# Block transposes on VectorE for one of the two forms of a triangular inverse, in place of matmuls

## The chip, the cores and the metric

The kernel runs on one core of one Trainium2 chip. The metric is the device time of one execution, in microseconds; 2361.78 us is the median of three runs of the kernel before. Most executions agree within 0.3%.

## What is computed

One inference step of a two-layer backbone. Each layer has a token mixer of three branches and a gated ConvFFN, over 128 context tokens and 256 latent tokens, 1024 channels wide, all in fp32. The change lies in the first branch, RWKV-7 time mixing, whose recurrence per head and direction is:

```
def step(S, inp):
    r_t, w_t, k_t, v_t, a_t, b_t = inp
    sa = jnp.einsum('bhvk,bhk->bhv', S, a_t)
    S = S * w_t[:, :, None, :] + sa[..., None] * b_t[:, :, None, :] + v_t[..., None] * k_t[:, :, None, :]
    return S, jnp.einsum('bhvk,bhk->bhv', S, r_t)
```

The kernel computes it in chunks of 64 tokens. Within a chunk the terms `sa` depend on each other through a strictly triangular 64x64 matrix L (products of `a_t` with earlier `b_s`, decayed), and what is needed is the inverse X = (I - L)^-1 for every chunk, head and direction. For the backward direction the triangle is the other one.

## The kernel before

**Stages.** The layer loop runs twice. In it, four head pairs `p` are worked through one after the other (the pair stage, about 137 us each), then come the merge, the output projection and the FFN as dense matmuls with split operands. Each engine has its own program, written in the order in which it runs; semaphores named in `PER` join them (`at_of(name, p, i)` is the i-th signal of that name in pair p). Nothing is reordered by a scheduler.

**Layout of the inverse.** A pair holds 2 heads (`hb`) x 6 combinations of direction and token tile (`x`) x 2 chunks (`c`), so 24 matrices of 64x64. The two chunks stand on the two halves of the 128 partitions. `xv` is X, `tvv` is its transpose, both `[128, hb, x, 64]` in SBUF, one `hb` being 128x384. `au[..., 0, 0:CH]` holds the transposed L after masking. `gg` is a scratch tile.

**The inverse by levels.** X starts as the identity. Level 0 writes the neighbours of the diagonal, and level `lv` (1 to 5, `LEVELS` = 6) joins diagonal blocks of size 2^lv into blocks of twice the size. For each level PE makes G = L X (`gl`, 24 matmuls, into PSUM), ACT copies it to `gg`, PE makes X G (side 0, `xt`) and its transpose G^T X^T (side 1), 24 matmuls each, and VectorE writes the new off-diagonal blocks into `xv` and `tvv` by a predicated copy (`pred`, L1210), one for each side and `hb`. Level 5 makes only side 1, since only `tvv` is read afterwards. For level 0 PE makes the not transposed L by 24 more matmuls (`l_done`), and GpSimd fills both `xv` and `tvv` with identities (L1553, L1554).

**What stands around it on each engine.** PE's order in a pair is: the products `am` (48 matmuls, masked by VectorE into `au`), the 24 for L, `attend(4)` of the attention branch, 24 for `g0`, then for each level: `gl`; other work (`attend`, transposes, and in levels 4 and 5 `retain` and `ada_steps`); then `xt`. So in time an `xt` group stands directly before the `gl` of the next level, which needs its result. VectorE runs `attend(4 + lv)` (or `retain(lv - 4)`) and then the four predicated copies of a level. ACT copies `gl` results, then its part of `attend`.

PE waits ahead of `gl` of level `lv`, for each `hb`, on the predicated copy of side 1 of the level before: index `4 * (lv - 1) + 2 * hb + 1` of `x_ready`.

**How the trace counts.** An fp32 matmul stands in the trace as two MATMUL records, so that the 24 + 24 + 24 matmuls of `xt` and the next `gl` are "x144". `settle()` makes an engine wait for its own previous instruction.

Of the kernel before, what the change touches and what calls it, by code (L numbers as in the profile page):

```python
# [27 lines left out]
P = 128  # L28
# [8 lines left out]
CH = 64  # L37
# [4 lines left out]
LEVELS = 6  # L42
# [33 lines left out]
for _name, _n in (("ident", 128), ("ones", 128), ("blk", 128), ("perm", 128), ("cos", 256), ("sin", 256),  # L76
# [6 lines left out]
PER = {  # L83
    "kk_rk": 1, "kk_sq": 1, "kkn_done": 1, "bon_done": 1, "bon_used": 1, "kkn_root": 1, "kk_ready": 1,
    "lw_done": 2, "la_done": 2, "sig_ready": 4, "scan_ready": 2, "lx_ready": 2, "exp_ready": 6, "kd_ready": 2,
    "til_ready": 2, "rr_ready": 2, "pend_ready": 2, "bkp_ready": 2, "dg_ready": 1, "x_init": 2, "bias_ready": 1,
    "vt_done": 1, "vt_ready": 1,
    "am_done": 6, "au_ready": 6, "l_done": 2, "x_ready": 22, "g0_done": 2, "g0_ready": 2,
    "gl_done": 10, "gl_ready": 10, "xt_done": 18, "wm_done": 2, "wm_ready": 2, "u_done": 2, "u_ready": 2,
    "mi_done": 2, "mi_ready": 2, "nn_done": 2, "nn_ready": 4, "qh_done": 2, "qh_ready": 4,  # L90
    "ch_done": 3, "ch_ready": 3, "yv_done": 2, "y_done": 2, "y_copied": 4, "yc_ready": 1, "ysq_ready": 1, "gn_done": 2,
    "yroot_ready": 1, "o_ready": 1,
# [41 lines left out]
def trunk(nc, xin, wstream, prm_d, pk_d, cc_d, const_d, x_out, nak, nav, srw, srt):  # L134
    ctx = ExitStack()
    with ctx:
# [151 lines left out]
        def sem(name):  # L288
# [9 lines left out]
            bias_ready bkp_ready bon_done bon_used c_ready ch_done ch_ready  # L298
            de_ready dg_ready dt_ready exp_ready g0_done g0_ready g_hi g_lo gelu_ready
            gl_done gl_ready gn_done h_hi h_lo h_ready half_used hnorm kd_ready kk_ready  # L300
            kk_rk kk_sq kkn_done kkn_root kt_done kt_ready l_done la_done lora_in lp_exp
            lw_done lx_ready m_hi m_lo mi_done mi_ready mod_ready mrg_ready mx_ready nn_done
            nn_ready no_done no_ready o_ready out_k out_st p_ready p_step pend_ready pk_in
            pn_ready prm_in pt_done pt_ready qh_done qh_ready qx_ready rgn_done ro_ready
            rope_done rope_ready row_done row_ready rows_clear rr_ready rroot_ready rsq_ready
            rst_done rst_ready rt_root ry_done ry_ready ryc_ready s_ready sc_done scan_ready
            sctx_ready sd_ready sig_ready silu_c sq_ready sq_used ss_done st0_ready st_done
            til_ready u_done u_ready v_step vt_done vt_ready w_hi w_lo w_used wm_done wm_ready
# [22 lines left out]
        with nc.Fori(0, DEPTH) as layer:  # L331
            with nc.Block() as block:
# [25 lines left out]
                def at_of(name, p, i):  # L358

                    return S[name].h, PER[name] * p + i + 1  # L360
# [4 lines left out]
                def hc(c):  # L365
                    return slice(CH * c, CH * c + CH)
# [44 lines left out]
                def _(pe):  # L411
                    used = [0]

                    def mm(out, a, b, start=True, stop=True, sig=None):
                        ins = nc.tensor.matmul(out, a, b, start=start, stop=stop, skip_group_check=True)  # L415
                        if sig:
                            S[sig].by(ins)
                        elif used[0]:
                            S["w_used"].by(ins, used[0])
                            used[0] = 0  # L420
# [79 lines left out]
                    for p in range(PAIRS):  # L500
# [125 lines left out]
                        for q in range(3):  # L626
# [5 lines left out]
                            for x in (2 * q, 2 * q + 1):  # L632
                                d, t = x // 3, x % 3
                                for k in range(2):
                                    for c in range(2):
                                        for hb in range(2):
# [1 line left out]
                                            mm(psw[hc(c), b, a:a + 128].rearrange("p (e i) -> p e i", e=2),  # L638
                                               bk[rows(hb), d, k, tok(t, c)], ar[rows(hb), d, :, tok(t, c)],
                                               sig="am_done" if (x % 2, k, c) == (1, 1, 1) else None)  # L640
                        pe.wait_ge(*at_of("au_ready", p, 3))
                        for x in range(6):
                            d, t = x // 3, x % 3
                            for c in range(2):
                                for hb in range(2):
                                    mm(psw[hc(c), 2 + hb, CH * x:CH * x + CH], ar[rows(hb), d, 0, tok(t, c)],
                                       bk[rows(hb), d, 0, tok(t, c)], sig="l_done" if (x, c) == (5, 1) else None)
                        attend(4)
                        for hb in range(2):
                            pe.wait_ge(*at_of("au_ready", p, 4 + hb))  # L650
# [4 lines left out]

                        for lv in range(1, LEVELS):
                            for hb in range(2):
                                pe.wait_ge(*at_of("x_ready", p, 4 * (lv - 1) + 2 * hb + 1))
                                for x in range(6):
                                    for c in range(2):  # L660
                                        mm(psw[hc(c), g_bank(lv, hb), CH * x:CH * x + CH], au[hc(c), hb, x, 0, 0:CH],
                                           xv[hc(c), hb, x, :], sig="gl_done" if (x, c) == (5, 1) else None)
                            if lv == 1:
                                attend(5)
                                for d in range(2):
                                    flipped(zb + 13 + d, [ar[:, d, 0, TT[t]:TT[t] + P] for t in range(3)])
                                pe.wait_ge(*at_of("g0_ready", p, 1))
                            elif lv in (2, 3):
                                d = lv - 2
                                attend(lv + 4)  # L670
                                pe.wait_ge(*at_of("bkp_ready", p, d))
                                for k in range(2):
                                    flipped(zb + 15 + 2 * d + k, [bkp[:, d, k, t * P:t * P + P] for t in range(3)])
                            else:
                                retain(lv - 4)
                                ada_steps(2)
                            for hb in range(2):
                                pe.wait_ge(*at_of("gl_ready", p, 2 * (lv - 1) + hb))
                                for side in range(1 if lv == LEVELS - 1 else 0, 2):
                                    b = g_bank(lv, hb) if side else x_bank(lv, hb)  # L680
                                    a_, b_ = (gg, tvv) if side else (tvv, gg)
                                    for x in range(6):
                                        for c in range(2):
                                            mm(psw[hc(c), b, CH * x:CH * x + CH], a_[hc(c), hb, x, :],
                                               b_[hc(c), hb, x, :], sig="xt_done" if (x, c) == (5, 1) else None)

                        freed(zb + 13)
                        freed(zb + 14)
                        for hb in range(2):
                            pe.wait_ge(*at_of("x_ready", p, 20 + hb))  # L690
# [499 lines left out]
                def _(dve):  # L1190
# [18 lines left out]
                    def pred(out, mask, data, sig):  # L1209
                        L.do(V.copy_predicated(out, mask, data), S[sig])  # L1210

                    def normed(j):

# [84 lines left out]
                    for p in range(PAIRS):  # L1298
# [91 lines left out]
                        for q in range(3):  # L1390
                            for hb in range(2):
# [7 lines left out]
                        dve.wait_ge(*at_of("x_init", p, 1))  # L1399
                        L.settle()  # L1400
                        for hb in range(2):
                            dve.wait_ge(*at_of("l_done", p, hb))
                            pred(by_dir(xv[:, hb]), level_mask(0, 0), by_dir_of(2 + hb), "x_ready")
                            pred(by_dir(tvv[:, hb]), level_mask(0, 1), by_dir(au[:, hb, :, 0, 0:CH]), "x_ready")
                        attend(4)
                        for lv in range(1, LEVELS):
                            if lv < 4:
                                attend(4 + lv)
                            else:
                                retain(lv - 4)  # L1410
                            for hb in range(2):
                                for side in range(1 if lv == LEVELS - 1 else 0, 2):
                                    i = 16 + hb if lv == LEVELS - 1 else 4 * (lv - 1) + 2 * hb + side
                                    dve.wait_ge(*at_of("xt_done", p, i))
                                    pred(by_dir((tvv if side else xv)[:, hb]), level_mask(lv, side),
                                         by_dir_of(g_bank(lv, hb) if side else x_bank(lv, hb)), "x_ready")
                            if lv == 2:
                                for hb in range(2):
                                    i = 8 + 2 * p + hb
                                    ts(dtab[:, hb, :], cv("posd", 384), lg[:, i:i + 1])  # L1420
                                    L.settle()
                                    stt(dtab[:, hb, :], cv("negd", 384), lg[:, i + 8:i + 9], dtab[:, hb, :], op1=ALU.add,
                                        sig="dt_ready")
# [96 lines left out]
                def _(pool):  # L1520
# [11 lines left out]
                    for p in range(PAIRS):  # L1532
# [17 lines left out]
                        pool.wait_ge(*at_of("til_ready", p, 1))  # L1550
                        eye = cv("eye", CH)
                        L.settle()
                        L.do(G.tensor_copy(xv.rearrange("p h x c -> p (h x) c"), eye.unsqueeze(1).to_broadcast([P, 12, CH])), S["x_init"])  # L1553
                        L.do(G.tensor_copy(tvv.rearrange("p h x c -> p (h x) c"), eye.unsqueeze(1).to_broadcast([P, 12, CH])), S["x_init"])  # L1554
                        pool.wait_ge(*at_of("pend_ready", p, 1))
                        for d in range(2):
# [172 lines left out]
```

## Time and profile before

| | us |
|---|---|
| median of 3 runs | 2361.78 (2360.79 to 2362.64) |
| the profiled execution | 2359.16 |
| its span, first to last instruction | 2357.4 |
| PE busy in the span | 2103.2 (89%) |
| VectorE busy | 968.0 (41%) |
| ACT busy | 855.0 (36%) |
| GpSimd busy | 661.6 (28%) |
| mean granted TensorE clock | 0.959 |

PE is the busiest engine by far, and its gaps are short. The share alone doesn't tell what one stage is limited by: the pair stage alternates between dense matmuls and chains of small steps in which PE, ACT and VectorE hand results on. Such chains are read in the timelines of the engines side by side. "Idle before" in a timeline row names the engine whose work ended that gap.

### The profile page before, as it was taken

The numbers are of one execution on the slowest core, as the hardware profiler recorded it, in microseconds if no ns is written. First come the engines' busy times: TensorE is split into PE (matmuls) and PEld (weight loads), VectorE is DVE, ScalarE is ACT, GpSimd is POOL, SyncE is SP. The second block draws the span as 40 slices with busy tenths as digits, with TensorE's granted clock in tenths as the row PEclk, the third lists the DMA queues.
The fourth block names the chain that finished last, engine by engine and source line by source line (L and its number), as shares of the span: only waits on it lengthen the run. The fifth ranks groups of instructions, "written<-read, shape, count | busy, mean of one in ns | idle before, by whom it ended". The sixth has DMA issues, their size and how long they took to land. (4 is left out here: it accounts for less than half of the span.)

```text
span 2357.4 us, 44798 instructions
## 1 busy us (share of the span) xinstructions
PE 2103.2 (89%) x18904; PEld 1696.5 (72%) x18904; DVE 968.0 (41%) x1589; ACT 855.0 (36%) x1668; POOL 661.6 (28%) x390
## 2 busy tenths in 40 slices
PE   4889999998799979999649899999987999799994
PEld 0566575756599959999615766757575999599994
DVE  2344435444443245650214444445545322455502
ACT  2342433334333344443133423333343333544431
POOL 0110202011155525555202002020201555255551
PEclk9999999999899979999879999999998999899997
DMA  6313222131233313333043131221312333133330
GB/s 239 105 38 116 66 77 97 39 116 38 88 121 122 120 54 118 125 124 125 18 174 117 36 112 61 92 91 56 100 38 93 117 125 120 59 120 124 123 125 27
DMA packets 64421, 227.37 MB, mean 96 GB/s; under 512 B 7264, under 2 KB 11616, under 8 KB 63840
## 3 DMA queue, kind: packets, MB, share of 16 engines
q1 hardware_dynamic: 58464, 215.60, 27.8%
q10 hardware_dynamic: 5760, 8.92, 1.2%
q8 instruction: 152, 2.49, 0.4%
q14 instruction: 45, 0.37, 0.1%
HBM read 220.81 MB, written 3.68 MB: 95 GB/s over the span
## 5 line engine op out<-in xcount | busy, mean ns | idle before, releaser
L415 PE MATMUL psz<-part 128*128 128x386 f32 x5280 | 959.3, 343 | 53.0 <-DVE part L1198 51.0
L415 PEld LDWEIGHTS psz<-part 128*128 128x128 f32 x5280 | 942.9, 191 | 66.0 <-issue 46.1
L1525 POOL TENSOR_TENSOR part<-ring,part 128x1024 fp32r<-128x1024 f32 x220 | 528.7, 2404 | 574.0 <-ACT part L856 574.0
L415 PE MATMUL psz<-hbuf,ring 128*128 128x386 f32 x1344 | 451.7, 493 | 31.7 <-issue 29.3
L415 PE MATMUL psw<-work 64*64 64x64 f32 (+5 forms) x10944 | 434.5, 234 | 31.2 <-issue 16.9
L415 PEld LDWEIGHTS psw<-work 64*64 64x64 f32 (+3 forms) x10944 | 381.0, 139 | 108.6 <-issue 80.7
L415 PEld LDWEIGHTS psz<-hbuf,ring 128*128 128x128 f32 x1344 | 254.2, 191 | 217.8 <-issue 39.5
L856 ACT ACTIVATE part<-ring 128x1024 fp32r<-128x1024 f32 x220 | 231.5, 1053 | 172.2 <-PE psz L415 155.8
L856 ACT ACTIVATE work<-psw 128x384 f32<-128x384 f32 (+6 forms) x360 | 129.6, 388 | 294.1 <-PE psw L415 248.6
L1525 POOL TENSOR_TENSOR work<-work 128x386 f32<-128x386 f32 (+1 forms) x48 | 42.6, 895 | 448.9 <-DVE work L1198 437.7
L1204 DVE SCALAR_TENSOR_TENSOR mix<-psz,prm,mix 128x385 f32<-128x385 f32 x176 | 109.0, 619 | 138.2 <-ACT mix L856 135.1
L1198 DVE TENSOR_TENSOR part<-mix,part 128x386 fp32r<-128x386 f32 x84 | 128.9, 1555 | 67.5 <-ACT part L856 67.5
L856 ACT ACTIVATE mix<-psz 128x386 f32<-128x386 f32 x96 | 47.3, 493 | 258.0 <-PE psz L415 252.8
L1207 DVE RECIPROCAL rstd<-rstd 128x386 f32<-128x386 f32 x8 | 20.5, 2564 | 265.0 <-ACT rstd L856 265.0
L1210 DVE COPY_PREDICATED work<-const,psw 128x384 f32<-128x384 uint32 x160 | 94.3, 591 | 76.6 <-PE psw L415 65.6
L856 ACT ACTIVATE mix<-psz,prm 128x386 f32<-128x386 f32 x88 | 51.4, 585 | 201.7 <-DVE mix L1198 104.5
L856 ACT ACTIVATE work<-psz 128x386 f32<-128x386 f32 (+2 forms) x160 | 75.7, 499 | 130.9 <-PE psz L415 127.5
L1198 DVE TENSOR_TENSOR work<-psw,work 128x256 f32<-128x256 f32 (+3 forms) x128 | 45.9, 395 | 152.8 <-PE psw L415 152.8
L1525 POOL TENSOR_TENSOR pk<-pk,const 128x768 f32<-128x768 f32 x8 | 14.6, 1826 | 290.2 <-DMA pk<-in_pk 290.2
L856 ACT ACT_TABLE_LOAD x58 | 74.4, 1283 | 49.6 <-issue 27.0
L415 PE MATMUL psw<-ring,small 128*2 128x512 f32 x128 | 35.1, 654 | 59.7 <-DMA ring<-in_w 59.2
L1198 DVE TENSOR_TENSOR mix<-psz,mix 128x386 f32<-128x386 f32 x48 | 26.7, 559 | 145.6 <-PE psz L415 145.5
(89 smaller groups left out, 1341.1 us busy)
## 6 DMA issues: line engine op xcount, KB each, us to landing
ring<-in_w SPq DMA_DIRECT2D x400, 512.0 KB, 3.5
pk<-in_pk ACTq DMA_DIRECT2D x8, 832.0 KB, 4.5
const<-in_const SPq DMA_DIRECT2D x1, 2307.0 KB, 8.2
xres<-in_x SPq DMA_DIRECT2D x1, 1544.0 KB, 11.2
out_x<-xres SPq DMA_DIRECT2D x1, 1544.0 KB, 5.1
out_nak<-work ACTq DMA_DIRECT2D x8, 64.0 KB, 1.5
out_nav<-work ACTq DMA_DIRECT2D x8, 64.0 KB, 1.5
out_srt<-work ACTq DMA_DIRECT2D x8, 64.0 KB, 1.5
```

Source lines behind the costliest of these rows:

```text
L415: ins = nc.tensor.matmul(out, a, b, start=start, stop=stop, skip_group_check=True)
L856: L.do(nc.scalar.activation(out, src, f, **kw), S[sig] if sig else None, free)
L1198: L.do(V.tensor_tensor(out, a, b, op), *sig_of(sig, free))
L1204: L.do(V.scalar_tensor_tensor(out, a, s_, b, op0, op1), *sig_of(sig, free))
L1207: L.do(V.reciprocal(out, a), *sig_of(sig, None))
L1210: L.do(V.copy_predicated(out, mask, data), S[sig])
L1525: L.do(G.tensor_tensor(out, a, b, op), S[sig] if sig else None)
```

## The change

The matrices L in not transposed form and the transposed products of levels 1 to 4 are no longer made by PE. In levels 0 to 4 the two forms are block diagonal with blocks of at most 32x32, and VectorE's transpose instruction turns every 32x32 block of a 128x384 tile in place of its block position. `flip` is that instruction. Level 0 now writes `tvv` by a predicated copy from `au` and makes `xv` by a flip; levels 1 to 4 write `xv` by a predicated copy and make `tvv` by a flip. Each flip waits for the copy ahead of it (`L.settle()`). Level 5 is as before but for its PSUM bank. A new semaphore `tv_ready` says that `tvv` is written, and `x_ready` that `xv` is; PE waits for `x_ready` ahead of `gl` and for `tv_ready` ahead of `xt`. GpSimd fills one tile with identities instead of two.

```diff
@@ PE
-                        pe.wait_ge(*at_of("au_ready", p, 3))
-                        for x in range(6):
-                            d, t = x // 3, x % 3
-                            for c in range(2):
-                                for hb in range(2):
-                                    mm(psw[hc(c), 2 + hb, CH * x:CH * x + CH], ar[rows(hb), d, 0, tok(t, c)],
-                                       bk[rows(hb), d, 0, tok(t, c)], sig="l_done" if (x, c) == (5, 1) else None)
...
-                                pe.wait_ge(*at_of("x_ready", p, 4 * (lv - 1) + 2 * hb + 1))
+                                pe.wait_ge(*at_of("x_ready", p, 2 * (lv - 1) + hb))
...
-                                for side in range(1 if lv == LEVELS - 1 else 0, 2):
-                                    b = g_bank(lv, hb) if side else x_bank(lv, hb)
-                                    a_, b_ = (gg, tvv) if side else (tvv, gg)
-                                    for x in range(6):
-                                        for c in range(2):
-                                            mm(psw[hc(c), b, CH * x:CH * x + CH], a_[hc(c), hb, x, :],
-                                               b_[hc(c), hb, x, :], sig="xt_done" if (x, c) == (5, 1) else None)
+                                if lv > 1:
+                                    pe.wait_ge(*at_of("tv_ready", p, 2 * (lv - 2) + hb))
+                                a_, b_ = (gg, tvv) if lv == LEVELS - 1 else (tvv, gg)
+                                for x in range(6):
+                                    for c in range(2):
+                                        mm(psw[hc(c), x_bank(lv, hb), CH * x:CH * x + CH], a_[hc(c), hb, x, :],
+                                           b_[hc(c), hb, x, :], sig="xt_done" if (x, c) == (5, 1) else None)
@@ VectorE
+                    def flip(out, a, sig):
+
+                        L.do(V.transpose(out.rearrange("p x c -> p (x c)"), a.rearrange("p x c -> p (x c)")), S[sig])
...
-                            dve.wait_ge(*at_of("l_done", p, hb))
-                            pred(by_dir(xv[:, hb]), level_mask(0, 0), by_dir_of(2 + hb), "x_ready")
-                            pred(by_dir(tvv[:, hb]), level_mask(0, 1), by_dir(au[:, hb, :, 0, 0:CH]), "x_ready")
+                            pred(by_dir(tvv[:, hb]), level_mask(0, 1), by_dir(au[:, hb, :, 0, 0:CH]))
+                            L.settle()
+                            flip(xv[:, hb], tvv[:, hb], "x_ready")
...
-                                for side in range(1 if lv == LEVELS - 1 else 0, 2):
-                                    i = 16 + hb if lv == LEVELS - 1 else 4 * (lv - 1) + 2 * hb + side
-                                    dve.wait_ge(*at_of("xt_done", p, i))
-                                    pred(by_dir((tvv if side else xv)[:, hb]), level_mask(lv, side),
-                                         by_dir_of(g_bank(lv, hb) if side else x_bank(lv, hb)), "x_ready")
+                                dve.wait_ge(*at_of("xt_done", p, 2 * (lv - 1) + hb))
+                                if lv == LEVELS - 1:
+                                    pred(by_dir(tvv[:, hb]), level_mask(lv, 1), by_dir_of(x_bank(lv, hb)), "tv_ready")
+                                    continue
+                                pred(by_dir(xv[:, hb]), level_mask(lv, 0), by_dir_of(x_bank(lv, hb)), "x_ready")
+                                L.settle()
+                                flip(tvv[:, hb], xv[:, hb], "tv_ready")
@@ GpSimd
-                        L.do(G.tensor_copy(xv.rearrange("p h x c -> p (h x) c"), eye.unsqueeze(1).to_broadcast([P, 12, CH])), S["x_init"])
```

VectorE from the `am` masks of a pair to `attend(4)`, before. COPY_PREDICATED is `pred`, TENSOR_TENSOR 128x512 the masking into `au`, RECIPROCAL the start of `attend(4)`:

```order
L1198 TENSOR_TENSOR work<-psw,const 128x512 x6
L1210 COPY_PREDICATED work<-const,psw 128x384
L1210 COPY_PREDICATED work<-const,work 128x384
L1210 COPY_PREDICATED work<-const,psw 128x384
L1210 COPY_PREDICATED work<-const,work 128x384
L1207 RECIPROCAL small<-small 128x1
```

The same place now; STREAM_TRANSPOSE is `flip`:

```order
L1191 TENSOR_TENSOR work<-psw,const 128x512 x6
L1203 COPY_PREDICATED work<-const,work 128x384
L1207 STREAM_TRANSPOSE work<-work 128x384
L1203 COPY_PREDICATED work<-const,work 128x384
L1207 STREAM_TRANSPOSE work<-work 128x384
L1200 RECIPROCAL small<-small 128x1
```

Two copies of four have become transposes, each directly behind the copy that it reads.

VectorE at level 2, before and now (the four copies of the level, `attend(6)` ahead of them, the decay tables behind):

```order
L1207 RECIPROCAL small<-small 128x1
L1201 TENSOR_SCALAR work<-work,small 128x384
L1210 COPY_PREDICATED work<-const,psw 128x384 x4
L1201 TENSOR_SCALAR work<-const,small 128x384
L1204 SCALAR_TENSOR_TENSOR work<-const,small,work 128x384
```

```order
L1200 RECIPROCAL small<-small 128x1
L1194 TENSOR_SCALAR work<-work,small 128x384
L1203 COPY_PREDICATED work<-const,psw 128x384
L1207 STREAM_TRANSPOSE work<-work 128x384
L1203 COPY_PREDICATED work<-const,psw 128x384
L1207 STREAM_TRANSPOSE work<-work 128x384
L1194 TENSOR_SCALAR work<-const,small 128x384
L1197 SCALAR_TENSOR_TENSOR work<-const,small,work 128x384
```

The second `hb`'s copy, for which PE waits, now stands behind the first `hb`'s transpose.

PE from the `am` products (64x128 x48) to `attend(5)`, before. The x24 are the matmuls for L, x48 are `g0` and `gl` of level 1, and x72 are the two sides of `xt` of a level and `gl` of the next:

```order
L415 MATMUL psw<-work 64x128 x48
L415 MATMUL psw<-work 64x64 x24
L423 MATMUL psw<-const,work 128x128 x3
L415 MATMUL psw<-work,pk 64x128
L415 MATMUL psw<-work 64x128 x2
L415 MATMUL psw<-pk,work 128x128
L415 MATMUL psw<-work 128x256
L415 MATMUL psw<-work 64x64 x48
L423 MATMUL psw<-const,work 128x128
```

The same place now:

```order
L415 MATMUL psw<-work 64x128 x48
L423 MATMUL psw<-const,work 128x128 x3
L415 MATMUL psw<-work,pk 64x128
L415 MATMUL psw<-work 64x128 x2
L415 MATMUL psw<-pk,work 128x128
L415 MATMUL psw<-work 128x256
L415 MATMUL psw<-work 64x64 x48
L423 MATMUL psw<-const,work 128x128
```

The matmuls for L stood between `am` and `attend(4)`; nothing stands there now. PE from `xt` of level 1 to `xt` of level 2, before and now:

```order
L423 MATMUL psz<-const,work 128x128 x6
L415 MATMUL psw<-work 64x64 x72
L423 MATMUL psw<-const,work 128x128 x3
L415 MATMUL psw<-work,pk 64x128
L415 MATMUL psw<-work 64x128 x2
L423 MATMUL psz<-const,work 128x128 x6
L415 MATMUL psw<-work 64x64 x72
```

```order
L423 MATMUL psz<-const,work 128x128 x6
L415 MATMUL psw<-work 64x64 x48
L423 MATMUL psw<-const,work 128x128 x3
L415 MATMUL psw<-work,pk 64x128
L415 MATMUL psw<-work 64x128 x2
L423 MATMUL psz<-const,work 128x128 x6
L415 MATMUL psw<-work 64x64 x48
```

Each of the four groups of 72 matmuls (`xt` of levels 1 to 4 with the next `gl`) is a group of 48.

## Rows read from the trace of the kernel before

**Rows 1.** The page: span and part 1 (busy us, share, instructions).

```profile
span 2357.4 us, 44798 instructions
...
PE 2103.2 (89%) x18904; PEld 1696.5 (72%) x18904; DVE 968.0 (41%) x1589; ACT 855.0 (36%) x1668; POOL 661.6 (28%) x390
```

**Rows 2.** Timeline, PE, pair 0, layer 0: start us, us, group, count, [idle before].

```profile
147.41 0.55 PE L423 MATMUL psw<-const,work 128*128 128x128 f32 x3
...
149.66 3.54 PE L415 MATMUL psw<-work 64*128 64x256 f32 x98
...
154.28 0.43 PE L415 MATMUL psw<-work 128*64 128x128 f32 x2 [0.82 <-ACT work L856]
...
156.30 4.62 PE L415 MATMUL psw<-work 64*64 64x64 f32 x144
...
163.59 4.62 PE L415 MATMUL psw<-work 64*64 64x64 f32 x144
168.14 0.55 PE L423 MATMUL psw<-const,work 128*128 128x128 f32 x3
...
177.56 5.90 PE L415 MATMUL psw<-work 64*64 64x64 f32 x150
```

**Rows 3.** Tile psw, PE, 163.5:168.2: ns min/median/max, first and last start.

```profile
L415 PE MATMUL psw<-work x144: 217/218/267, 163.6 to 168.0; 64*64 64x64 f32 x144
```

**Rows 4.** Timeline, DVE, the same stretch and columns.

```profile
147.97 0.59 DVE L1210 COPY_PREDICATED work<-const,psw 128x384 f32<-128x384 uint32 x1
148.45 0.59 DVE L1210 COPY_PREDICATED work<-const,work 128x384 f32<-128x384 uint32 x1
...
149.86 0.17 DVE L1207 RECIPROCAL small<-small 128x1 f32<-128x1 f32 x1
...
150.61 0.42 DVE L1198 TENSOR_TENSOR work<-psw,pk 128x256 f32<-128x256 f32 x1 [0.26 <-ACT work L856]
...
164.55 2.69 DVE L1210 COPY_PREDICATED work<-const,psw 128x384 f32<-128x384 uint32 x4 [4.10 <-PE psw L415]
167.13 0.41 DVE L1201 TENSOR_SCALAR work<-const,small 128x384 f32<-128x384 f32 x1
...
178.67 2.54 DVE L1210 COPY_PREDICATED work<-const,psw 128x384 f32<-128x384 uint32 x4
```

**Rows 5.** Timeline, ACT, the same stretch and columns.

```profile
151.84 0.62 ACT L856 ACTIVATE work<-work,small 128x384 f32<-128x384 f32 x1 [1.26 <-DVE small L1201]
...
152.45 1.78 ACT L856 ACTIVATE work<-psw 128x384 f32<-128x384 f32 x5
...
163.37 0.87 ACT L856 ACTIVATE work<-psz 128x384 f32<-128x384 f32 x2 [0.20 <-PE psz L423]
...
168.26 0.96 ACT L856 ACTIVATE work<-psw 128x384 f32<-128x384 f32 x2 [0.42 <-PE psw L415]
...
182.22 0.49 ACT L856 ACTIVATE work<-psw 128x384 f32<-128x384 f32 x1 [0.41 <-PE psw L415]
```

**Rows 6.** Groups by shape: count | busy us, mean ns | idle us before.

```profile
L1207 DVE RECIPROCAL work<-work 128x386 f32<-128x386 f32 x24 | 61.5, 2563 | 20.2 <-ACT work L856 19.9
...
L1354 DVE TENSOR_REDUCE small<-work 128x1 f32<-128x384 f32 x32 | 17.7, 553 | 1.1
...
L1201 DVE TENSOR_SCALAR work<-work,small 128x384 f32<-128x384 f32 x32 | 13.5, 421 | 1.1
...
L1210 DVE COPY_PREDICATED work<-const,work 128x384 f32<-128x384 uint32 x16 | 9.3, 581 | 0.0
...
L1354 DVE TENSOR_REDUCE small<-work 128x1 f32<-128x128 f32 x16 | 4.6, 286 | 49.8 <-ACT work L856 49.8
```

**Rows 7.** Stretches of pairs 0 and 1, busy us by engine, clock, DMA.

```profile
core 0: us, PE busy (x) PEld busy (x) DVE busy (x) ACT busy (x) POOL busy (x), PEclk, DMA share, GB/s
...
163.60:171.00 7.40, 6.82 (x164) 6.04 (x165) 4.24 (x8) 2.71 (x7) 0.00 (x0) 1.00 0.01 2
280.00:294.00 14.00, 12.54 (x266) 10.78 (x266) 8.18 (x18) 4.85 (x16) 0.00 (x0) 0.88 0.02 4
```

More of the change, by code:

```diff
@@ L85 @@
     "lw_done": 2, "la_done": 2, "sig_ready": 4, "scan_ready": 2, "lx_ready": 2, "exp_ready": 6, "kd_ready": 2,
-    "til_ready": 2, "rr_ready": 2, "pend_ready": 2, "bkp_ready": 2, "dg_ready": 1, "x_init": 2, "bias_ready": 1,
+    "til_ready": 2, "rr_ready": 2, "pend_ready": 2, "bkp_ready": 2, "dg_ready": 1, "x_init": 1, "bias_ready": 1,
     "vt_done": 1, "vt_ready": 1,
-    "am_done": 6, "au_ready": 6, "l_done": 2, "x_ready": 22, "g0_done": 2, "g0_ready": 2,
-    "gl_done": 10, "gl_ready": 10, "xt_done": 18, "wm_done": 2, "wm_ready": 2, "u_done": 2, "u_ready": 2,
+    "am_done": 6, "au_ready": 6, "x_ready": 10, "tv_ready": 10, "g0_done": 2, "g0_ready": 2,
+    "gl_done": 10, "gl_ready": 10, "xt_done": 10, "wm_done": 2, "wm_ready": 2, "u_done": 2, "u_ready": 2,
     "mi_done": 2, "mi_ready": 2, "nn_done": 2, "nn_ready": 4, "qh_done": 2, "qh_ready": 4,
@@ L300, in trunk @@
             gl_done gl_ready gn_done h_hi h_lo h_ready half_used hnorm kd_ready kk_ready
-            kk_rk kk_sq kkn_done kkn_root kt_done kt_ready l_done la_done lora_in lp_exp
+            kk_rk kk_sq kkn_done kkn_root kt_done kt_ready la_done lora_in lp_exp
             lw_done lx_ready m_hi m_lo mi_done mi_ready mod_ready mrg_ready mx_ready nn_done
@@ L307, in trunk @@
             sctx_ready sd_ready sig_ready silu_c sq_ready sq_used ss_done st0_ready st_done
-            til_ready u_done u_ready v_step vt_done vt_ready w_hi w_lo w_used wm_done wm_ready
+            til_ready tv_ready u_done u_ready v_step vt_done vt_ready w_hi w_lo w_used wm_done wm_ready
             x_init x_ready x_upd xi_ready xt_done y_copied y_done yc_ready yroot_ready yv_done
@@ L689, in _ @@
                         for hb in range(2):
-                            pe.wait_ge(*at_of("x_ready", p, 20 + hb))
+                            pe.wait_ge(*at_of("tv_ready", p, 8 + hb))
                             for x in range(6):
@@ L1207, in recip, with pred @@
                         L.do(V.reciprocal(out, a), *sig_of(sig, None))
-                    def pred(out, mask, data, sig):
-                        L.do(V.copy_predicated(out, mask, data), S[sig])
+                    def pred(out, mask, data, sig=None):
+                        L.do(V.copy_predicated(out, mask, data), S[sig] if sig else None)
+                    def flip(out, a, sig):
+                        L.do(V.transpose(out.rearrange("p x c -> p (x c)"), a.rearrange("p x c -> p (x c)")), S[sig])
                     def normed(j):
@@ L1398, in _ @@
                                    w((2 * q + hb) % 4, 0, 512).rearrange("p (x k c) -> p x k c", x=2, k=2), m, sig="au_ready")
-                        dve.wait_ge(*at_of("x_init", p, 1))
+                        dve.wait_ge(*at_of("x_init", p, 0))
                         L.settle()
                         for hb in range(2):
-                            dve.wait_ge(*at_of("l_done", p, hb))
-                            pred(by_dir(xv[:, hb]), level_mask(0, 0), by_dir_of(2 + hb), "x_ready")
-                            pred(by_dir(tvv[:, hb]), level_mask(0, 1), by_dir(au[:, hb, :, 0, 0:CH]), "x_ready")
+                            pred(by_dir(tvv[:, hb]), level_mask(0, 1), by_dir(au[:, hb, :, 0, 0:CH]))
+                            L.settle()
+                            flip(xv[:, hb], tvv[:, hb], "x_ready")
                         attend(4)
```

## The prediction

> **What bounds the kernel now.** I read the page first: PE is busy for 2103.2 of 2357.4 us [rows 1], so what leaves PE can count, if the other engines let PE move up. Then I read the pair stage by the timelines of PE, VectorE and ACT side by side, since the edits all lie there, in 8 passes (2 layers, 4 pairs). PE's rows show a level as a period of 7.29 us: group x144 at 156.30, the next at 163.59 [rows 2]. The group itself fills 4.55 us, from 163.59 to the transposes at 168.14; the rest is attention work with short waits for ACT. Level 4 to 5 has the same size: ACT's copy of the last `gl` starts 4.67 us after the group (168.26 after 163.59) and in level 4 4.66 us after it (182.22 after 177.56) [rows 2, 5].
>
> Within a group, PE does 24 records per `hb` and side. VectorE starts its first copy 0.96 us after the group's start (164.55), and its four copies end at 167.24 [rows 2, 4]. They are paced by PE: between two is (2.69 - 0.59) / 3 = 0.70 us, so 24 records take 0.70 us on PE, and a result is seen 0.26 us after that. 144 records would be 4.20 us, and the last starts at 168.0, 4.4 us after the first [rows 3]. So PE already waits about 0.2 us for the fourth copy ahead of the last `gl`, and what follows on PE starts 0.90 us after that copy's end (168.14 - 167.24). The matmul chain and the copy chain are nearly even. A change that takes PE work away meets VectorE's chain at once.
>
> **What goes from PE.** 24 matmuls (48 records) in each of 4 levels: 2 x 0.70 = 1.40 us by PE's own time. 24 matmuls for L as well: they lie ahead of 147.41, where `attend(4)` starts [rows 2]. If PE were the only limit this would be 4 x 1.4 = 5.6 us for the levels alone, 45 us over 8 pairs. I take that as a bound and not as the sum.
>
> **What VectorE's chain makes of a level.** Let d be the duration of one flip, and count from the first `xt` matmul. First copy 0.96 to 1.55. Its flip waits for it; dependent steps follow each other after 0.04 us in these rows, so it starts at 1.59. The next copy doesn't read it, and unlike the flip it may start before the one ahead has ended: copies without a wait between them start every 0.47 to 0.48 us at 0.59 long [rows 4], so 0.11 us of the end is overlapped. It starts at 1.48 + d and ends at 2.07 + d. Its `xt` result has been there since 2 x 0.70 + 0.26 = 1.66. Then the same 0.90 as before, so PE goes on at 2.97 + d, where it was 4.55. Gain: **1.58 - d**, for the three transitions from levels 1, 2 and 3. From level 4, VectorE does `retain(0)` first and starts its copies at 178.67, 1.11 us after the group (177.56) [rows 2, 4], 0.15 later than in the others, while its old end was the same (178.67 + 2.54 - 177.56 = 3.65). Gain: **1.43 - d**.
>
> **Level 0.** VectorE's copies start at 147.97, right behind the masks, not behind the L matmuls. `attend(4)` on VectorE starts at 149.86, reaches the 128x256 addition at 150.61 after 0.26 us of waiting, and ACT's exponential waits for it (151.84), then the copies of `g0`, `gl` and the probabilities run on ACT without a gap from 152.45, and PE waits for the last of them until 154.28 [rows 2, 4, 5]. So this chain, not PE, sets when level 1 starts, and the time of the L matmuls becomes waiting. Now: copy 147.97, flip 148.60, copy 148.49 + d, flip 149.12 + d, `attend(4)` at 149.01 + 2d, addition 0.49 later (0.75 less the wait of 0.26), at 149.50 + 2d against 150.61. Gain: **1.11 - 2d**, about nothing. PE's `g0` and `gl` (from 149.66, now earlier) cover both flips.
>
> **The sum as a function of d.** 3 x (1.58 - d) + (1.43 - d) + (1.11 - 2d) = **7.28 - 6d** per pair.
>
> **What d is.** No row shows a transpose. From below: the 128x384 TENSOR_SCALAR, 0.421 us; from above the slowest kind in the trace, RECIPROCAL 128x386, 2.563 us. Nearest by work (SBUF to SBUF, 384 fp32 elements per partition, no arithmetic) is the copy predicated from `au`, 0.581; TENSOR_REDUCE, which reads the same 384, takes 0.553 [rows 6]. The two reductions give 267 ns for 256 elements more, about one element per ns, and 0.15 us fixed. TENSOR_SCALAR runs through its elements faster than that; I see no reason why a reordering step would. I take d = 0.59. Then 3.74 us per pair, 29.9 us over 8. With d = 0.42 it is 4.76, 38 us; with 2.56 a loss of 8.08, 65 us.
>
> The Trainium skill's page "VectorE: DVE Perf Modes", section "The three transpose paths", gives 311 ns for a 128x128 transpose on VectorE in bf16. Worked on with the slope of the reductions to 384 columns, that would be an estimate of 0.58 us and 30 us in all; fp32 is not in its table.
>
> **What else moves, at nothing.** The `tv_ready` waits of `xt`: the second flip ends at 2.11 + 2d = 3.3, and the next `xt` starts after 2.97 + d and 2.74 us of other work. ACT's copies of the transposed tiles end at 163.37 + 0.87, long ahead of the next `gg` copy, also when that comes 1 us earlier [rows 5]. VectorE's decay tables stand behind level 2's flips, which end sooner than the fourth copy did; 1.0 us of that cover is gone only for d over 1.0. One GpSimd fill less, far ahead of its readers. DMA is at a share of 0.01 in these stretches [rows 7], so a shorter stage meets no transfer. What stands behind level 5 keeps its distances.
>
> The time before is the median, 2361.78; the profiled execution took 2359.16 with its span of 2357.4, so the sum carries over as it is: 2361.8 - 29.9 = **2332**.
>
> **Rivals.**
>
> *The flip is half as fast per element.* Then it is 0.15 + 2 x 0.40 = 0.95 us, the gain 7.28 - 5.7 = 1.58 per pair, 13 us: 2349. For it: no row shows how 4-byte elements are reordered. Against: all plain fp32 rows run at one element per ns or faster.
>
> *The next instruction can't overlap a flip's end.* Then each of the six steps behind a flip (four in the levels, two in level 0) starts 0.11 us later: 0.66 per pair, 5.3 us, 2337. For it: a flip passes its data in another order than a copy. Against: the copies of rows 4 do overlap, as does the step from copy to reciprocal. The Trainium skill, "VectorE: DVE Perf Modes", section "The DRAIN you can't avoid", says that the next operation starts only when the pipe has emptied, unless it isn't held; by the first half of that rule this rival holds. The rows at level 0 disagree with it for copies.
>
> *The clock falls.* PE waits more in these stages: it is idle for 0.6 of 7.4 us in the levels [rows 7], and would be for about 1.0 of 6.3. In the trace the granted clock is 1.00 in the levels and 0.88 over 14 us in the stretch of pair 1 that begins with the `am` products, behind a wait for ACT [rows 7]; between its two levels, 2.4 and 1.2 GHz, that is 0.12 x 14 = 1.7 us lost at most. One more such stretch in each pair would cost 13 us: 2345. Against: PE stays busy for over four fifths.
>
> *The flip is long, and the kernel is slower.* The place is the chain copy, flip, copy ahead of `gl`: PE waits for the second `hb`'s copy, which stands behind the first's flip on VectorE. It decides from d = 7.28 / 6 = 1.21 us on. With RECIPROCAL's 2.56 it is 2361.8 + 65 = 2426. For it: VectorE has a row of over 6 ns per element. Against: that one computes, a flip doesn't.
>
> *No change*: d between 1.12 and 1.31, by chance.
>
> **How the numbers follow.** Forecast with or without overlap, 2322 to 2341: 0.74. Half as fast: 0.11. Clock: 0.05. Long flip: 0.06. No change: 0.04. The range takes in the forecast's lower bound, d = 0.42 (2324, and 2 us for the median), and above it half speed and the clock: 2322 to 2350. A difference under 0.2%, 4.7 us, can't be told from none; faster than that 0.90, within 0.04, slower 0.06.
>
> **What would show it.** In the profile after: STREAM_TRANSPOSE x80 with a mean near 590 ns; the period of the levels down from 7.29 to about 6.3; the groups x144 now x96, with PE waiting for VectorE inside them; `attend(5)` of PE starting at the same distance behind the `am` masks, with a longer wait ahead; VectorE's busy time about as before, and PE's down by some 1900 records. Wrong would be: a flip far from 0.59, copies that start late behind flips, ACT as the releaser of `xt`, or a clock under 1.00 in the levels.

## The result and the profile after

The changed kernel takes 2335.6 us (median of 4 runs, 2334.8 to 2336.4), the kernel before 2362.2 beside it: a ratio on record of 0.9894, 95% interval 0.988 to 0.9908 (the two medians divide to 0.9887). It is 26.6 us faster, where 29.9 were forecast (2332). The profiled execution took 2336.4 us, its span fell by 22.8 us, from 2357.4 to:

```profile
span 2334.6 us, 41014 instructions
...
PE 2067.2 (89%) x16984; PEld 1654.9 (71%) x16984; DVE 956.7 (41%) x1589; ACT 854.5 (37%) x1668; POOL 655.7 (28%) x382
```

PE lost 1920 MATMUL records against [rows 1] and 36 us of busy time. VectorE has as many instructions as before. The price that no row of before showed, d, stands in the groups by shape (count | busy us, mean ns of one | idle before):

```profile
L1207 DVE STREAM_TRANSPOSE work<-work 128x384 f32<-128x384 f32 x80 | 46.4, 579 | 2.7
L1203 DVE COPY_PREDICATED work<-const,psw 128x384 f32<-128x384 uint32 x80 | 46.1, 576 | 62.0 <-PE psw L415 60.8
```

A flip takes 0.58 us, as long as a predicated copy [rows 6]. Next the levels, in PE's timeline of pair 0 (start us, us, group, count, idle before):

```profile
159.75 0.43 PE L415 MATMUL psw<-work 128*64 128x128 f32 x2 [1.63 <-ACT work L849]
...
161.77 2.53 PE L415 MATMUL psw<-work 64*64 64x64 f32 x72
164.47 0.92 PE L415 MATMUL psw<-work 64*64 64x64 f32 x24 [0.18 <-DVE work L1203]
165.32 0.55 PE L423 MATMUL psw<-const,work 128*128 128x128 f32 x3
...
168.05 2.52 PE L415 MATMUL psw<-work 64*64 64x64 f32 x72
```

The period of a level is now 168.05 - 161.77 = 6.28 us, for 7.29 in [rows 2]. From the first `xt` to the transposes behind `gl` it is 165.32 - 161.77 = 3.55 us, for 4.55. PE's own work would have allowed 1.40 less, and 1.0 came: the second `gl` group (x24) starts late, released by VectorE. On VectorE the same stretch reads:

```profile
153.50 0.60 DVE L1203 COPY_PREDICATED work<-const,work 128x384 f32<-128x384 uint32 x1
154.14 0.58 DVE L1207 STREAM_TRANSPOSE work<-work 128x384 f32<-128x384 f32 x1
154.64 0.55 DVE L1203 COPY_PREDICATED work<-const,work 128x384 f32<-128x384 uint32 x1
...
156.08 0.42 DVE L1191 TENSOR_TENSOR work<-psw,pk 128x256 f32<-128x256 f32 x1
...
162.74 0.59 DVE L1203 COPY_PREDICATED work<-const,psw 128x384 f32<-128x384 uint32 x1 [0.15 <-PE psw L415]
163.36 0.58 DVE L1207 STREAM_TRANSPOSE work<-work 128x384 f32<-128x384 f32 x1
163.86 0.55 DVE L1203 COPY_PREDICATED work<-const,psw 128x384 f32<-128x384 uint32 x1
```

Copy, flip and copy start at 162.74, 163.36 and 163.86: the flip 0.62 us after the copy that it reads, the next copy 0.50 after the flip starts, so it does overlap the flip's end. It ends at 164.41, and PE's waiting `gl` starts at 164.47. In level 0 the attention addition comes 156.08 - 153.50 = 2.58 us after the first copy, for 2.64 in [rows 4]. All of this is the forecast's chain to about 0.1 us.

What isn't: this chain makes about 31 us, and the profiled span fell by 22.8. The mean granted clock fell from 0.959 to 0.952. Read over the eight pair stages, the clock is at its lower level for 23.9 us in all before and for 54.6 us after. As 18 us of pair 1, from about the first `am` product on (columns as in [rows 7]), before and then after:

```profile
core 0: us, PE busy (x) PEld busy (x) DVE busy (x) ACT busy (x) POOL busy (x), PEclk, DMA share, GB/s
280.00:298.00 18.00, 16.54 (x392) 14.55 (x394) 11.61 (x26) 6.44 (x21) 0.00 (x0) 0.91 0.02 4
```

```profile
281.00:299.00 18.00, 14.98 (x268) 12.87 (x270) 10.16 (x22) 6.87 (x23) 0.00 (x0) 0.81 0.01 4
```

With 1.2 and 2.4 GHz as the levels, 0.91 is 3.2 us at the lower one and 0.81 is 6.8. The low stretches begin at two places. The first is at the `am` products, within 1.5 us of the first of them, behind or in a wait of 2.1 us; there the clock is low for 23.9 us before and for 34.1 after. The second is behind PE's wait ahead of `attend(5)`, 12 to 14 us after the first `am` product, and from there the low stretch reaches into level 1; before has none there, after has 20.5 us, in pairs 1, 2, 5 and 6. In pair 2 the second place stands alone. First the kernel before, then the changed one, 11 us each from 8 us behind the first `am` product on, then PE's row at that wait:

```profile
426.00:437.00 11.00, 10.18 (x256) 8.73 (x254) 5.93 (x15) 5.18 (x15) 0.00 (x0) 1.00 0.01 3
```

```profile
425.00:436.00 11.00, 9.30 (x147) 7.89 (x145) 4.98 (x14) 4.60 (x14) 0.00 (x0) 0.69 0.01 1
```

```profile
428.34 0.43 PE L415 MATMUL psw<-work 128*64 128x128 f32 x2 [1.70 <-ACT work L849]
```

The second place is where the L matmuls left PE: this wait was 0.82 us [rows 2] and is now 1.6 to 1.8 (1.63 in row 159.75 above).

### The profile page after: what moved, and what is told of

Read it like the earlier page. It is cut to its first block and busy times, and to the rows that moved or that the text cites. A ratio compares the mean times of both kernels' runs of the same rounds, so it can differ in the third digit from the quotient of the medians.

```text
span 2334.6 us, 41014 instructions
## 1 busy us (share of the span) xinstructions
PE 2067.2 (89%) x16984; PEld 1654.9 (71%) x16984; DVE 956.7 (41%) x1589; ACT 854.5 (37%) x1668; POOL 655.7 (28%) x382
## 5 line engine op out<-in xcount | busy, mean ns | idle before, releaser
L415 PE MATMUL psw<-work 64*64 64x64 f32 (+3 forms) x9024 | 398.3, 242 | 43.2 <-ACT work L849 18.5
L415 PEld LDWEIGHTS psw<-work 64*64 64x64 f32 (+2 forms) x9024 | 340.6, 143 | 123.4 <-issue 80.7
L1200 DVE RECIPROCAL rstd<-rstd 128x386 f32<-128x386 f32 x8 | 20.5, 2564 | 264.9 <-ACT rstd L849 264.9
L1191 DVE TENSOR_TENSOR work<-work 128x386 f32<-128x386 f32 (+1 forms) x120 | 75.5, 655 | 3.3
```

Source lines behind the costliest of these rows:

```text
L1191: L.do(V.tensor_tensor(out, a, b, op), *sig_of(sig, free))
```

## The experiments

Theory 1 is that of the forecast: the chain copy, flip, copy on VectorE sets the levels, and level 0 is neutral. Theory 2 came with the trace after: the L matmuls cost nothing on the path, but they kept the clock up, and without them low stretches take part of the gain back. Its rival is that the low stretches fell otherwise by the shift in time alone. "Low clock" below is the sum over the eight pair stages of the profiled execution.

The kernel before ran again beside each set of experiments: 2361.0 us beside e1 to e4, 2359.6 beside e5 to e8, 2359.7 beside e9 to e11, for 2362.2 beside the changed kernel. So a difference between kernels of two sets is uncertain by some 2.5 us.

**e1_levels_only.** Level 0 by the L matmuls and two copies for each `hb`, as in the kernel before but with the two copies in the other order; flips in levels 1 to 4.

```diff
+                        pe.wait_ge(*at_of("au_ready", p, 3))
+                        ... the 24 matmuls for L, sig="l_done"
-                            L.settle()
-                            flip(xv[:, hb], tvv[:, hb], "x_ready")
+                            dve.wait_ge(*at_of("l_done", p, hb))
+                            pred(by_dir(xv[:, hb]), level_mask(0, 0), by_dir_of(2 + hb), "x_ready")
```

> Flips in levels 1 to 4 alone; L from PE and two copies for level 0, as in the kernel before. Theory 1 (the copy and flip chain sets the levels, level 0 is neutral): undisturbed, a pair gains 3 x 1.01 + 0.86 = 3.9 us as in the changed kernel. Theory 2, on top of it (the low-clock stretches around the masks grew from 24 to 55 us in all because PE lost the L matmuls there): the low stretches go back to about 24 us and the time is 2325 to 2331. Rival (they grew by the shift of the timing alone): low stretches stay near 55 us and the time within 2 us of the changed kernel's 2335.6.

Measured: 2327.0 us (2322.6 to 2331.1), ratio 0.9866 (0.9836 to 0.9896). Low clock 13.7 us. Half of the change is 8.6 us faster than the whole: level 0's part costs time. All of this run's low clock lies at the first place.

**e2_level0_only.** The other half: level 0 by flips, without the L matmuls; levels 1 to 4 as in the kernel before.

> Level 0 by flips, without the L matmuls; levels 1 to 4 as in the kernel before, with both sides on PE. Theory 1: the chain through VectorE's attention step is as long as before, so within 2 us of the kernel before by itself. Theory 2: the low stretches grow, and the kernel is 4 to 10 us slower than before, 2366 to 2372. Rival: the 24 L matmuls were on the path, 1.0 us a pair, and it is 8 us faster, 2354.

Measured: 2369.4 us, ratio 1.0034 (1.002 to 1.0048), 8.4 us slower than the kernel before beside it (2361.0). Low clock 51.2 us. In the profile, 18 us of pair 1 from about the first `am` product on, with all of its levels still as before:

```profile
285.00:303.00 18.00, 15.00 (x268) 12.63 (x270) 9.67 (x21) 6.88 (x23) 0.00 (x0) 0.81 0.02 6
```

Taking 192 matmuls out of the program, and two copies a pair for flips, made it slower. The chain isn't the reason: in pair 0, where the clock was up in level 0, VectorE's first copy of level 1 starts 9.23 us behind that of level 0, for 9.29 in the kernel before. The rival that the matmuls were on the path (2354) is out.

**e3_l_matmuls_kept.** The changed kernel with the L matmuls left in; their result is read by nobody.

```diff
+                        pe.wait_ge(*at_of("au_ready", p, 3))
+                        ... the 24 matmuls for L, sig=None
```

> The changed kernel with the 24 matmuls for L left in on PE, their result read by nobody. Theory 2: PE waits for ACT there in any case, so they cost nothing, and they keep the clock: low stretches about 24 us, 2325 to 2331. Rival (the low stretches hang on the timing): 2334 to 2338. If the matmuls were on the path: 2343.

Measured: 2328.0 us (2325.3 to 2328.7), ratio 0.9861 (0.9832 to 0.9889). Low clock 27.3 us, half of the changed kernel's. Unread work in a wait made the kernel 7.6 us faster, or 6.5 if each is taken against the kernel before beside it. Up to here the kernels without the L matmuls (changed, e2) have over 50 us of low clock, and those with them (before, e1, e3) under 28. But only the second place follows the L matmuls: it has 20.5 us in the changed kernel, 23.9 in e2 and nothing in the other three. At the first place the clock is low for 34.1, 27.3, 23.9, 13.7 and 27.3 us in these five, with and without them, and PE's work and waits ahead of it in the pair are the same in all five. So theory 2 holds for the second place, and for the first place the rival does.

**e4_two_flips.** Each flip done twice.

```diff
+                        L.do(V.transpose(out.rearrange("p x c -> p (x c)"), a.rearrange("p x c -> p (x c)")))
+                        L.settle()
                         L.do(V.transpose(out.rearrange("p x c -> p (x c)"), a.rearrange("p x c -> p (x c)")), S[sig])
```

> The changed kernel with each flip done twice, the second waiting for the first, so d grows by 0.58 + 0.04 = 0.62 us. Theory 1: a pair loses (4 + 2) x 0.62 = 3.7 us, 30 us in all, 2365. Rival (part of the flips is covered, as in level 0 by PE's and ACT's own work): 4 x 0.62 x 8 = 20 us, 2355.

Measured: 2374.3 us, ratio 1.0062 (1.004 to 1.0085), 38.7 us over the changed kernel. The levels do as expected; PE in level 3 of pair 1:

```profile
314.40 2.53 PE L415 MATMUL psw<-work 64*64 64x64 f32 x72
317.71 0.92 PE L415 MATMUL psw<-work 64*64 64x64 f32 x24 [0.78 <-DVE work L1203]
318.56 1.13 PE L415 MATMUL psw<-work,const 128*128 128x256 f32 x4
```

From 314.40 to 318.56 is 4.16 us, 0.61 more than 3.55, and PE's wait for the second copy is 0.78 for 0.18. The term of d in the levels is right. Level 0 in pair 0, VectorE's first copy and PE at `attend(5)`:

```profile
149.36 0.59 DVE L1203 COPY_PREDICATED work<-const,work 128x384 f32<-128x384 uint32 x1
156.83 0.69 PE L415 MATMUL psw<-work 128*64 128x128 f32 x2 [2.72 <-ACT work L849]
```

`attend(5)` comes 156.83 - 149.36 = 7.47 us behind the copy, for 159.75 - 153.50 = 6.25 in the changed kernel: 1.22 us, twice the 0.61. So the term 2d of level 0 holds as well, and the rival that part of the flips is covered (20 us) is out. The total came out 9 us over the 30 expected, and the low clock rose to 71.7 us, 44.4 of it at the second place.

**e5_copies_first.** Both copies of a level ahead of both flips.

```diff
                                 pred(by_dir(xv[:, hb]), level_mask(lv, 0), by_dir_of(x_bank(lv, hb)), "x_ready")
-                                L.settle()
+                            for hb in range(2 if lv < LEVELS - 1 else 0):
+                                dve.wait_ge(*at_of("x_ready", p, 2 * lv + hb))
                                 flip(tvv[:, hb], xv[:, hb], "tv_ready")
```

> The changed kernel with both predicated copies of a level (1 to 4) ahead of both flips on VectorE. Theory 1: the flip leaves the chain that PE waits for; the second copy then starts when its product is there (1.66 us after the group's start, not 2.09), the level period goes from 6.28 to about 5.87, 1.6 us a pair, 13 us: 2323 if the low-clock stretches stay at 55 us. Rival: the flips are then late for the next xt product or for the attention step behind them, and the period stays at 6.28: 2336.

Measured: 2325.8 us (2322.4 to 2330.9), ratio 0.986 (0.984 to 0.9881), 9.8 us under the changed kernel. Low clock 51.2 us. PE, then VectorE in pair 0:

```profile
160.84 3.23 PE L415 MATMUL psw<-work 64*64 64x64 f32 x96
164.01 0.55 PE L423 MATMUL psw<-const,work 128*128 128x128 f32 x3
...
166.74 3.23 PE L415 MATMUL psw<-work 64*64 64x64 f32 x96
```

```profile
161.81 1.30 DVE L1203 COPY_PREDICATED work<-const,psw 128x384 f32<-128x384 uint32 x2
162.99 1.02 DVE L1207 STREAM_TRANSPOSE work<-work 128x384 f32<-128x384 f32 x2
```

The period is 5.90 us for 6.28. The flips (162.99 to 164.01) run while PE makes the last `gl`, ahead of the attention work at 164.01; the copy that PE waits for no longer stands behind one. So the flip in that chain cost 0.38 us a level, as theory 1 says. The matching gain of 12 us came as 10, or as 7 against the kernels before beside the two; the low clock was 3.4 us less as well, and this gap wasn't followed further.

**e6_filler.** The changed kernel with matmuls of the identity, unread, in the 2.1 us wait ahead of `am`.

```diff
                         pe.wait_ge(*at_of("bon_used", p, 0))
+                        for i in range(12):
+                            mm(w(2, 0, P), ident, ident)
                         pe.wait_ge(*at_of("vt_ready", p, 0))
```

> The changed kernel with 12 matmuls of the identity by itself (128x128, result unread) on PE in the 2.1 us wait ahead of the am products. Theory 2: that wait is what the clock falls behind, the low stretches of the pair stages mostly vanish, and the time falls by up to 16 us: 2320 to 2325. Rival (the waits in level 0, behind the am products, matter): low stretches remain, 2330 to 2336.

Measured: 2333.2 us (2330.2 to 2338.0), ratio 0.9891 (0.987 to 0.9911): 2.4 us, inside the spread. Low clock 41.0 us. The expectation failed. No low stretch begins at the `am` products any longer, but the second place now has one in every pair; in pair 1 it runs from about 293 to 296.4 us, 12 us behind the first `am` product and just behind PE's wait ahead of `attend(5)`. And 12 fillers are too many: `am` starts 24.61 us after GpSimd's identity fill, for 24.12 in the changed kernel, 4 us over eight pairs. Low clock also costs more at the second place: pairs of the changed kernel with 6.8 us there alone lose 2.45 us, those with 6.8 us at the first place alone lose 1.7. So 13.7 us less of low clock brought next to nothing. Either wait alone lets the clock fall.

**e8_before_filler and e9_after_no_low_clock.** The kernel before with the same fillers, and the changed kernel with the fillers and the L matmuls kept.

> The kernel before with the same 12 filler matmuls. Theory 2: its 24 us of low clock in the pair stages vanish, 6 us less: 2355. It is the undisturbed base: between it and the filled changed kernel stand the 32 us that the chain theory gives. Rival (the filler itself costs time on the path): 2361 or more.

> The changed kernel with the 12 filler matmuls and the L matmuls kept unread, its order of copies and flips untouched. Against the kernel before with the same filler (2353.9) it is the change with the clock held. The chain theory gives 3 x 1.01 + 0.86 = 3.9 us a pair, 31 us: 2323, with no low clock in the pair stages. If the sum of the prediction hides an error of its own: outside 2320 to 2326.

Measured: 2353.9 us (2352.4 to 2359.2), ratio 0.998 (0.9971 to 0.999), and 2327.6 us (2324.0 to 2330.6), ratio 0.9869 (0.9852 to 0.9887). e8 came as expected. The median of e9 lies 1.6 us outside the 2320 to 2326 that its expectation allowed, though its profiled execution (2324.0) lies inside. Neither profile has low clock in any pair stage, so these two show the change undisturbed. GpSimd's identity fills of pairs 1 and 2, in e8 and then e9 (start, us), give the length of a whole pair stage:

```profile
258.36 0.82 POOL L1555 COPY work<-const 128x768 f32<-128x768 f32 x1 [1.42 <-DVE work L1200]
...
396.14 0.82 POOL L1555 COPY work<-const 128x768 f32<-128x768 f32 x1 [1.42 <-DVE work L1200]
```

```profile
254.54 0.82 POOL L1561 COPY work<-const 128x768 f32<-128x768 f32 x1 [1.42 <-DVE work L1200]
...
388.31 0.82 POOL L1561 COPY work<-const 128x768 f32<-128x768 f32 x1 [1.42 <-DVE work L1200]
```

137.78 and 133.77 us. The other distances between fills of one layer are 137.67 or 137.68 in e8 and 133.77 to 133.83 in e9, but for 134.83 in pair 0 of e9, where the extra 1 us lies behind the inverse. The part of the pair stage that the change touches, from the fill to the last copy of level 5, is 3.9 us shorter in each of the 8 pairs, 31 us in all. The two profiled spans also differ by 31.4 us (2353.6 and 2322.2), but in part by chance: the profiled execution was the fastest of the four of e9 and 1.5 us above the median of e8. The medians differ by only 26.3. The three slower executions of e9 were granted a clock of 0.961 to 0.962, the profiled one 0.964; where they lost time isn't recorded. Part of the scatter between kernels lies ahead of pair 0, where the first fill comes at 118.4 to 122.8 us.

**e7_all_three and e10_all_8_fillers.** Copies first, L matmuls kept, 12 fillers, then 8.

> Copies first, the filler ahead of am, and the L matmuls kept unread. If both theories hold: 2335.6 - 13 - 16 = 2307, with a granted clock of 1.00 through the pair stages. If the clock then falls in the shorter levels instead, 2315 or more.

> Copies first, L matmuls kept, and 8 filler matmuls in place of 12. The am products start 0.5 us later behind 12, so 8 should fit the wait: up to 4 us less than 2310.2, so 2306, if the clock holds with fewer. If it doesn't: low stretches come back, 2310 or more.

Measured: 2310.2 us (2308.2 to 2314.2), ratio 0.9791 (0.9774 to 0.9807), and 2309.1 us (2305.9 to 2312.1), ratio 0.9784 (0.9764 to 0.9804). No low clock in the pair stages of either; 8 fillers hold it as well and fit the wait (`am` starts at 24.06 us after the fill). A pair stage is 132.24 and 131.71 us. The medians show 1 of the 4 us that this makes. This is the fastest version: 26.5 us under the changed kernel, or 24.1 against the kernels before beside the two.

**e11_attend_first.** As e10, and in level 0 `attend(4)` on VectorE between the two copies and the two flips.

> The kernel with 8 fillers, and in level 0 VectorE's attend(4) between the two copies and the two flips. The exponential on ACT then starts earlier and the g and probability copies behind it; PE's wait of 0.8 to 1.6 us ahead of attend(5) shrinks by some 0.4 us a pair: 3 us less than with 8 fillers. Rival (the gl products of level 1 then wait for the flips and ACT's copies for them): same or slower.

Measured: 2314.2 us (2310.2 to 2317.1), ratio 0.9808 (0.9787 to 0.9828), 5 us over e10 with overlapping runs; but in its trace VectorE's first copy of level 1 starts 9.71 us after that of level 0 in each pair, for 9.28 in e10. PE in pair 0:

```profile
156.38 1.61 PE L415 MATMUL psw<-work 64*64 64x64 f32 x48 [0.54 <-DVE work L1216]
...
158.76 0.43 PE L415 MATMUL psw<-work 128*64 128x128 f32 x2 [0.50 <-ACT work L858]
```

The rival holds: the `gl` products of level 1 now wait for the second set of instructions, the flips (0.54 us). VectorE's attention addition couldn't start earlier, since it waited 1.20 us for ACT.

## Why the forecast was right, point by point

**d.** Forecast 0.59, measured 0.579. The nearest row by work, a copy between the same tiles, was the right one to take; both ends of the range (0.42, 2.56) were far off. The Trainium skill's "VectorE: DVE Perf Modes", section "The three transpose paths", gives 311 ns for 128x128 in bf16. The prediction's estimate of 0.58 us, worked out from that and from the slope of the reductions, agrees with the trace, though no run here transposes bf16. The rivals of a half-speed and of a long flip fall with it.

**The levels.** With d = 0.58 the forecast gives 1.00 for three transitions and 0.85 for the fourth. Measured without low clock (e8 against e9): VectorE's first copies of levels 1, 2, 3 and 5 start 9.29, 16.58, 23.86 and 37.33 us behind that of level 0, against 9.27, 15.55, 21.82 and 33.41. That is 1.01 for each of the first two and 1.88 for the last two together. e4 and e5 show that it is the flip in the chain that limits them.

**Level 0.** Forecast -0.05 at this d, measured +0.02. e4 shows its dependence on d: 0.61 more for each flip made `attend(5)` 1.22 us later. That the L matmuls cost no time on the path is shown by e3.

**Overlap behind a flip.** The rival without it was worth 2337, nearer to the measured 2335.6 than the forecast. It is wrong all the same: the copy starts 0.50 us behind the flip's start. The Trainium skill's "VectorE: DVE Perf Modes", section "The DRAIN you can't avoid", says first that the next operation waits until the pipe is empty, and then that one which isn't held starts earlier; for a copy behind a transpose the trace agrees with the second half. A total that fits is no evidence for a mechanism.

**The clock.** This is the term that was missing from the sum. I had it as a rival, with 0.12 x 14 = 1.7 us at most for a further stretch and 13 us in all, but placed it in the levels, where PE's share falls. No low stretch began there; those of pairs 1, 2, 5 and 6 began ahead of level 1 and ran some 3 to 4 us into it, so one of the signs of being wrong that I named, a clock under 1.00 in the levels, did show. I wrote that the time of the L matmuls "becomes waiting" and priced that wait at nothing. In the profiled executions the pair stages from the identity fill to the last copy of level 5 sum to 548.9 us before and 527.3 after; with the clock up they would be 8 x 67.82 and 8 x 63.94, so low clock takes 6 us before and 16 after. The 10 us between are the gap between the chain's 31 and the 22 seen in the pair stages. About 7 of them come from the second place, the wait that I priced at nothing: pairs 2 and 6, with low clock there alone, are each 2.45 us over 63.94, and pairs 1 and 5 lose about 1 us each behind level 0's first copy. The rest comes from the first place, where the same work was at low clock for 34.1 us instead of 23.9; nothing in the change explains that but the moment at which each pair comes. In the medians the gap is about 5 us, as the four runs of the changed kernel ran 0 to 1.6 us faster than the profiled one, and those of before 1.6 to 3.5 us slower. That the forecast's 29.9 stands within 3.3 us of the measured 26.6 is in part luck: the two profiled executions differ by only 22.8.

The two places and what sits in the two waits, over all profiles (low clock of the eight pair stages, us):

| kernels | fillers ahead of `am` | L matmuls | first place | second place |
|---|---|---|---|---|
| before, e1, e3 | no | yes | 23.9, 13.7, 27.3 | 0 |
| changed, e2, e4, e5 | no | no | 34.1, 27.3, 27.3, 27.3 | 20.5, 23.9, 44.4, 23.9 |
| e6 | yes | no | 0 | 41.0 |
| e7 to e11 | yes | yes | 0 | 0 |

The second place occurs in 31 of 40 pairs without the L matmuls and in none of 64 with them.

**At nothing.** The `tv_ready` waits, ACT's copies, the decay tables, GpSimd and DMA gave no new releaser in the timelines after. This part held.

## What to carry to other kernels

When two engines hand results to each other in a chain, removed work is worth only the slack to the other engine's chain: here 1.0 of 1.4 us a level. Put next in order what the other engine waits for, and off-path work behind it (copies ahead of flips: 0.38 us a level). Matmuls that are off the path may still be worth their place where they fill a wait, since TensorE's clock fell behind waits; count low clock place by place before and after, and test each wait with unread matmuls.

## What the runs showed of the hardware

Leaving 24 off-path matmuls a pair in the changed kernel, unread, brought its low clock in the pair stages from 54.6 to 27.3 us and its time down by 7.6 us (e3). The lower level came at two places: at the `am` products, behind waits of PE of 0.69 and 2.12 us, and behind the waits of 0.58 and 1.6 to 2.7 us in level 0; PE was busy for 15.0 of 18 us around them. With the second of the waits in level 0 at 0.82 us it didn't come there, and in the levels, with waits of 0.18 and 0.58 us a period, no low stretch began. Eight or twelve unread matmuls in the first wait together with the 24 ahead of level 0 held the clock at its upper level in all eight pairs (e7 to e11); twelve in the first wait alone left 41.0 us at the second place, and the 24 alone left 13.7 to 27.3 at the first. Why the low stretches of one kernel differ between pairs with the same work, 0 to 6.8 us in the kernel before, stays open.

A block transpose of 128x384 fp32 elements in SBUF took 0.58 us, like a predicated copy of the same size, and a following instruction that didn't wait for it started 0.08 us ahead of its end.
